# Activation tables loaded ahead, two norms moved to VectorE, and three constants of the planner, in a hybrid decoder layer on eight cores

## The reference

```
h      = rmsnorm(x) @ w_in                       # 1024 -> 512 + 512 + 512 + 1024 + 1024
a      = h[:, :512];  u, v = gelu(h[:, 512:1536])
p      = (causal window sums of a, windows 2, 4, 8, 16, minus a) @ w_pool, per group
s      = u * (causal 128x128 mix of rmsnorm(v) by w_s + b_s)
merged = sigmoid(gate_a) * (p @ w_pool_out) + sigmoid(gate_b) * (s @ w_gmlp_out)
x      = x + merged @ w_out
h2     = rmsnorm(x)
x      = x + (silu(h2 @ w_gate) * (h2 @ w_up)) @ w_down      # d_ff 2816
y      = rmsnorm(x)
```

## Time and profile before

| | us |
|---|---|
| median of 3 runs (776.41 to 777.02) | 776.97 |
| the profiled execution, its own time | 777.7 |
| its span on the slowest core, core 5 | 776.1 |
| spans of the other cores | 771.0 to 776.0 |
| TensorE busy | 742.0 (96%) |
| DVE, ACT, POOL busy | 538.4, 354.5, 107.2 |

### The profile page before, as it was taken

How to read it: one execution, slowest core, us unless ns; L and a number is a source line. 1 busy time by engine, 2 the same in 40 slices (tenths; PEclk the granted TensorE clock), 3 DMA queues, 4 the chain that set the end, 5 groups by cost and what they waited for, 6 DMA issues and landing times.

```text
span 776.1 us, 14774 instructions; the slowest of 8 cores (771.0 to 776.1 us)
## 1 busy us (share of the span) xinstructions
PE 742.0 (96%) x4855; PEld 435.8 (56%) x4855; DVE 538.4 (69%) x1164; ACT 354.5 (46%) x753; POOL 107.2 (14%) x185
## 2 busy tenths in 40 slices
PE   5999999999999999999999999999999999999995
PEld 2664555666666654446656665445665666654442
DVE  2788868667666656766568758965577566768986
ACT  3587654544444445675545552001554555531222
POOL 4245111001000011120121001000111000002111
PEclk9999999999999999999999999999999999999998
DMA  8998704015223249573599205861385332005652
GB/s 204 242 246 187 159 27 57 1 15 82 42 29 42 28 86 281 123 142 90 94 197 139 36 10 76 271 213 29 55 133 91 50 42 42 1 1 186 224 192 109
DMA packets 46715, 82.92 MB, mean 107 GB/s; under 512 B 20288, under 2 KB 20416, under 8 KB 46624
## 3 DMA queue, kind: packets, MB, share of 16 engines
q0 software_dynamic: 15984, 29.11, 26.0%
q1 hardware_dynamic: 30222, 52.28, 23.0%
q10 hardware_dynamic: 434, 0.60, 0.2%
HBM read 87.83 MB, written 19.49 MB: 138 GB/s over the span
## 4 chain that ended last, share of the span: by engine, by line
PE 76%; issue 6%; DVE 6%; ACT 5%; DMA 4%; POOL 2%; DVEq 0%; ACTq 0%; POOLq 0%
PE ps L546 74%; ACT junk L567 3%; POOL rs L691 2%; DMA Sx<-wpk 2%; DMA Rg<-wpk 2%; DVE X L578 2%; ACT Sx L567 1%; DVE Pr L578 1%; ACT Fr L567 1%; DVE X L586 1%; PE ps L723 1%; DMA Mr<-wpk 1%; PE ps L1071 1%; DVE hT L578 1%; DVE Sx L578 0%
## 5 line engine op out<-in xcount | busy, mean ns | idle before, releaser
L567 ACT ACTIVATE Fr<-ps 128x344 f32<-128x344 f32 (+2 forms) x394 | 180.2, 465 | 203.0 <-PE ps L546 188.0
L578 DVE TENSOR_TENSOR Fr<-Fr,ps 128x344 f32<-128x344 f32 (+2 forms) x366 | 179.7, 508 | 109.0 <-ACT Fr L567 71.5
L546 PE MATMUL ps<-hT,Rg 128*128 128x344 f16 x1440 | 245.8, 309 | 5.5 <-ACT Fr L567 5.5
L546 PE MATMUL ps<-Sx,Rg 128*128 128x344 f16 x1080 | 189.9, 309 | 2.3 <-DVE Fr L578 1.5
L546 PEld LDWEIGHTS ps<-hT,Rg 128*128 128x128 f16 x1440 | 139.4, 98 | 78.8 <-issue 11.0
L546 PEld LDWEIGHTS ps<-Sx,Rg 128*128 128x128 f16 x1080 | 103.2, 98 | 59.3 <-issue 10.3
L578 DVE TENSOR_TENSOR X<-X,ps 128x512 f32<-128x512 f32 (+1 forms) x121 | 80.5, 682 | 26.0 <-PE ps L546 23.6
L567 ACT ACTIVATE Fr<-Fr 128x344 f16<-128x344 f32 x138 | 67.3, 488 | 54.5 <-DVE Fr L578 52.6
L546 PE MATMUL ps<-Mr,Pr 128*128 128x512 f16 x352 | 82.0, 379 | 2.4 <-DVE X L578 2.2
L611 POOL DMA_DIRECT2D Rg<-wpk x60 | 31.9, 532 | 374.5 <-PE ps L546 374.1
L567 ACT ACTIVATE junk<-X 128x1025 f16<-128x1025 f32 (+3 forms) x43 | 43.9, 1022 | 78.3 <-DVE X L578 73.1
(11 more groups left out here) (116 smaller groups left out, 575.6 us busy)
## 6 DMA issues: line engine op xcount, KB each, us to landing
Rg<-wpk POOLq DMA_DIRECT2D x60, 256.0 KB, 4.9
X<-xp SPq DMA_DIRECT2D x22, 512.0 KB, 13.4
X<-xd SPq DMA_DIRECT2D x18, 512.0 KB, 4.7
Mr<-wpk POOLq DMA_DIRECT2D x34, 256.0 KB, 8.7
yp<-X SPq DMA_DIRECT2D x14, 512.0 KB, 2.9
xd<-Pr SPq DMA_DIRECT2D x12, 512.0 KB, 6.1
Pr<-xp SPq DMA_DIRECT2D x10, 512.0 KB, 10.2
xd<-X SPq DMA_DIRECT2D x8, 512.0 KB, 5.4
```

What stands on the lines that cost most here:

```text
L546: ins = e.matmul(out=ap, lhsT=l, rhs=rr, start=(start and i == 0), stop=(stop and i == len(pairs) - 1), skip_group_check=more)
L567: return e.activation(out=P.r(out), in_=P.r(in_), func=func, scale=scale, **kw)
L578: return P.add(eng, lambda e: e.tensor_tensor(out=P.r(out), in0=P.r(a), in1=P.r(b), op=op), reads=[a, b], writes=[out], dur=vdur(n, per), ...
```

## The change

Five edits.

- Before the gate stage one activation of eight elements with Sigmoid is added on ACT, to run after all GELUs; all sigmoids run after it. Before the FFN one with SiLU, after all sigmoids; the SiLUs run after it. Both have priority -8 and are planned at 1400 ns.
- The power step of `rstd` is planned at 850 ns with a delay of 300 for priorities of 100 and more (560 and 150 before), and at 560 with 200 below.
- The first two norms are scaled on DVE, as the others are.
- Weights with a priority under 0.35 (the a, v and u units) count as landed 1000 ns later in the plan.
- A queue that turns active while the other has work is held for the full `LAG` in the plan.

```diff
+HSL = 1000.0
...
         if not self.q[i]:
-            self.gate[i] = self.t + min(self.left(1 - i), LAG)
+            self.gate[i] = self.t + (LAG if self.q[1 - i] else 0.0)
...
-                fin.done = rings.t + LAND
+                fin.done = rings.t + LAND + fin.slack
...
         def load(u, ap, sem, prio, after=()):
             where[u] = ap
-            return dma('pool', ap, wpk[UIDX[u], :, :], sem, rows(128, 4096), prio, after)
+            o_ = dma('pool', ap, wpk[UIDX[u], :, :], sem, rows(128, 4096), prio, after)
+            o_.slack = HSL if prio < 0.35 else 0.0
+            return o_
...
-                  dur=560.0, lat=150.0, prio=-6.0)
+                  dur=(560.0 if prio < 100.0 else 850.0), lat=(200.0 if prio < 100.0 else 300.0), prio=-6.0)
...
-        sca = lambda t: t < 2
+        sca = lambda t: False
...
+        gelus = []
+        sigs = []
+
+        def table(func, done):
+            o_ = act(tmp16[0:1, 0:8], mhalf[0:1, 0:1].to_broadcast([1, 8]), func, -8.0, n=8)
+            o_.dur = 1400.0
+            o_.preds = sorted(set(o_.preds) | set(q.i for q in done))
+            return o_
+
+        def follow(o_, pre):
+            o_.preds = sorted(set(o_.preds) | {pre.i})
+            return o_
...
+        sig0 = table(AF.Sigmoid, gelus)
...
-                    act(h[2], v, AF.Sigmoid, pr, n=WJ)
+                    sigs.append(follow(act(h[2], v, AF.Sigmoid, pr, n=WJ), sig0))
...
-                    act(s, t, AF.Sigmoid, pr, n=WJ)
+                    sigs.append(follow(act(s, t, AF.Sigmoid, pr, n=WJ), sig0))
...
+        sil0 = table(AF.Silu, sigs)
...
-                    act(h[0], t1, AF.Silu, pr, n=WJ)
+                    follow(act(h[0], t1, AF.Silu, pr, n=WJ), sil0)
...
-                    act(h[2], v, AF.Silu, pr, n=WJ)
+                    follow(act(h[2], v, AF.Silu, pr, n=WJ), sil0)
```

More of the change, by code:

```diff
@@ L92 @@
     __slots__ = ('i', 'eng', 'fn', 'dur', 'lat', 'prio', 'preds', 'succs', 'npred', 'pts', 'alloc',
-                 'dma', 'nbytes', 'start', 'end', 'done', 'seq', 'clock', 'waits', 'val', 'margin', 'loose')
+                 'dma', 'nbytes', 'start', 'end', 'done', 'seq', 'clock', 'waits', 'val', 'margin', 'loose', 'slack')
 class Rings:
@@ L200, in add @@
         o.loose = loose
+        o.slack = 0.0
         o.pts = []
@@ L796, in v_tile @@
             fv[0] = 1 - fi
-            act(Fb[:R, fi, 0:512], PV(pt, lambda p: p[:R, :]), AF.Gelu_apprx_tanh, prio)
+            gelus.append(act(Fb[:R, fi, 0:512], PV(pt, lambda p: p[:R, :]), AF.Gelu_apprx_tanh, prio))
             r = rstd(Fb[:R, fi, 0:513], R, 512.0 ** -0.5, prio)
@@ L822, in u_sample @@
             fs = Fb[:, fi, 0:64]
-            act(fs, PV(pt, lambda p: p[:, 0:64]), AF.Gelu_apprx_tanh, prio, n=64)
+            gelus.append(act(fs, PV(pt, lambda p: p[:, 0:64]), AF.Gelu_apprx_tanh, prio, n=64))
             def trs(e, p):
@@ L860, in u_stage @@
             fu[0] = 1 - fu[0]
-            act(Fb[:, fi, :W], PV(pt, lambda p: p[:, :W]), AF.Gelu_apprx_tanh, prio)
+            gelus.append(act(Fb[:, fi, :W], PV(pt, lambda p: p[:, :W]), AF.Gelu_apprx_tanh, prio))
             ps = PT()
@@ L1134, in build_nc @@
                 xstore(t, 2200.0 + n_, tlast)
-        fs = [0]
+        sil0 = table(AF.Silu, sigs)
         def ffn_unit(row, j, B, pr):
```

## The result

The changed kernel takes 768.06 us (median), the kernel before 776.69 in the same comparison: the ratio is 0.9882, 95% interval 0.9864 to 0.9899, so 1.2% faster, which is 9.2 us by the ratio; the two medians are 8.6 apart. The forecast was 773.2 with a range down to 769.5. The direction was right, the size was not: more than twice the gain. All comparisons are with runs of the kernel before on the same chip. Ratios, intervals and means of spans leave out the runs in which some cores ran at a lower clock and took some per cent longer; medians are over all runs.

What follows compares the result with a forecast made beforehand. TensorE's own work was taken to set the time, so only its standstills could change it. Sigmoid 1.0, SiLU 1.28, start 1.5 and power step 0 summed to 3.8 us, from 776.97 to 773.2; range 769.5 to 776.7.

Steps and rivals of the forecast that it cites:

- Sigmoid: Gate start: table load leaves the stretch between sum and first sigmoid; 1.0 us of TensorE's 1.30 us wait gained.
- SiLU: FFN start: table load moves behind the last sigmoid, copies come earlier; 1.28 us of TensorE's 2.83 us wait gained.
- The row and the page: Table loads: trace rows show 1.28 us per switch; the skill's page adds a 1.38 us drain, 2.66 in all.
- Start: First stage: norms on DVE, later weights and queue rule bring tile 1 earlier and remove TensorE's waits; 1.5 us gained.
- The rival that has the start given back: First stage paced by transfers, so only the tables pay: 2.3 us gained, 774.7 us; chance 0.24.
- Power step: Tail: longer planned step doesn't flip the order; taken at 0, with up to 1.9 us gained or lost.
- The larger gain by more flips: FFN start and tail: SiLU and copies precede the last scaling, three tail waits go; 7.3 us, 769.7; chance 0.10.
- ACT parked on x: First stage: squares planned ahead of copies make ACT wait for x, 3.9 us each; two give 781.0; chance 0.10.
- Renamed waits: Gate, FFN and first stage: other waits replace those removed; about 0.5 us gained, 776.5; chance 0.14.

Runs made afterwards that it cites:

- e17: The kernel before with the SiLU table activation alone; 775.04 us, ratio 0.9953.
- e18: The kernel before with 15 matmuls put on TensorE ahead of the group that waits at the FFN's start; 776.36 us, ratio 0.9983.
- e4: The kernel before with the three first-stage edits alone (norms on DVE, weights later, held queue rule); 777.60 us, ratio 0.9999.
- e2: The kernel before with the longer planned power step alone; 771.93 us, ratio 0.9928.
- e14: The kernel before with the power step planned longer in the FFN's final norm alone; 775.00 us, ratio 0.9965.
- e15: The kernel before with the power step planned as in the full change everywhere but in the final norm; 774.36 us, ratio 0.9950.
- e13: The kernel before with both table activations and the longer planned power step, without the three first-stage edits; 768.80 us, ratio 0.9887.
- e3: The kernel before with both table activations (Sigmoid and SiLU) alone; 772.67 us, ratio 0.9933.
- e1: The changed kernel with the power step planned as before (560 ns, delay 150); 773.64 us, ratio 0.9946.
- e16: e13 with the power step planned at 1460 ns instead of 850 for priorities of 100 and more; 767.09 us, ratio 0.9856.

## Why the prediction was right and wrong

**Sigmoid: right.** Taken at 1.0, measured 1.23 on all cores. The cover that I named, four groups on pooled data, is there. The table load moved behind the first copy, not ahead of it, so even the later copy for which I set 0.3 aside didn't come.

**SiLU: the mechanism right, the term mis-sized.** "So of 2.83 us I take 1.28." It measured 2.9 in the mean of the spans (e17): the wait itself fell by 1.43, a wait for a tile before it by 0.30, and the clock behind it gave back about 1 us more (e18). I had read one core, on which the clock didn't fall; the metric takes the slowest of eight. The upper end of 2.83, by which SiLU and copies come before the last scaling, didn't come: they stand behind it in every kernel.

The row and the page that I set against each other are told apart by this: the two loads are worth 1.23 and 1.43 us where the load stood, next to 1.28 for the load by itself. The Trainium skill ("ScalarE: Activation LUTs", "What ACT_TABLE_LOAD costs") puts a load at 2.66 with a drain of 1.38; no run here shows the drain.

**Start: wrong.** "The two together should take away the waits for activations, 0.83 + 0.69 = 1.5 us." It gave nothing (e4), and the waits themselves stayed, 0.82 and 1.18 on core 0 of after. Tile 1 came earlier, but the step from there to the u weights failed: I held 1.8 us to be free by the landing of one weight, while the squares on ACT wait for x, and through them the copies, TensorE at 31.86, and the first use of the weight, which is not before 38.5 but at 38.8 in after and 39.3 in e4. The rival that has the start given back was right on the start; its total of 774.7 was not. That old and new rule agree for the rest of the program, as I assumed, held: kernels with and without the start edits have the same lists behind the first 103 us.

**Power step: the step that failed.** "The order does not flip, so I take 0, with up to 3 x 0.65 = 1.9 gained or as much lost." It was worth 5.1 to 5.6 us alone (e2). I compared when the scaling is due with one thing, the addition behind it, and the addition indeed didn't pass it. The planner compares the scaling with everything that is ready on DVE, and a sum for a later group was: laid out 0.44 us later, the scaling comes behind that, and TensorE's order changes with it (e14, 2.2 us). I also set the times of the trace against each other where the planner has its own; in those the margin was 0.04 us, and had the step been planned 0.05 shorter, TensorE's order and my 0 would have stood in the tail. The fourth wait there, 1.42 us, I didn't see. And I looked for the effect in the tail alone, while the same step stands before the scalings of the first stage and the second norm (2.9 us, e15).

**Rivals.** The larger gain by more flips, at one chance in ten, had the mechanism in the tail, with 769.7 as its time; the flip at the FFN's start, SiLU and copies ahead of the scaling, is not how the rest came. ACT parked on x had its mechanism too: it happens in every kernel with the start edits. But its price was too high: with up to 12.2 us of such waits, and all else that the start edits do, e4 isn't slower. Renamed waits is right for the start alone. The sum of what was measured, Sigmoid 1.2, SiLU 2.9 and the power step 5.1, is 9.2 and by chance the same as the measured gain: the parts share 1.3 of it, and the changed kernel has 1.3 less than e13, of which 0.8 are the last stores. The mean of the spans fell by 9.7.

## What to carry to other kernels

Where a static planner lays out the order, look at waits on an operation whose estimate is below what the trace shows (0.56 planned, 0.71 on average, 1.46 beside DVE): other ready work may stand behind it. Correct the estimate for that operation alone and look at every place where it stands, not at the largest. Such a planner needs no chip: play it through with the new estimate and compare the orders of all engines before you put a term at 0, and mind how near a flip is to not happening. Price a long wait of TensorE at more than its length when the work behind it runs at a lower granted clock on any core, and look at all cores for that, since the slowest sets the time. A lead at the start of a stage is no gain until it reaches the stage's end: follow it through what the stage waits for, here the landing of x as well as of the weights.

## What was not expected of the hardware

The clock of TensorE differed between cores that ran the same instructions with the same wait: behind 2.8 us of idleness it fell on 13 of 24, behind 2.4 us on 7 of 16. A second such place is near 73 us, where the mix of the u stage waits for DVE twice in short order; on core 7 of the kernel before TensorE's waits there are 1.15 and 0.33 us, and the next 4 us have a granted clock of 0.57:

```profile
74.08 0.38 PE L546 MATMUL ps<-Mr 128*128 128x512 f16 x1 [1.15 <-DVE Pr L578]
74.79 2.15 PE L546 MATMUL ps<-Mr 128*128 128x512 f16 x6 [0.33 <-DVE Pr L578]
```

```profile
75.00:79.00 4.00, 4.00 (x12) 1.33 (x11) 2.08 (x4) 4.00 (x9) 2.11 (x4) 0.57 1.01 204
```

Waits of this kind there (1.15 to 1.19 and 0.33 to 0.38 us) are followed by the lower clock on 7 of the 40 cores of before, e3, e14, e17 and e18, two of them in the kernel before (1.5 to 1.7 us each), and on none of the 56 of the other kernels with a profile (after, e1, e2, e4, e13, e15 and e16). In e2 and e15 that may be part of the gain of the longer power step; it is read from the traces and no run tried it by itself.

The last two stores land in 2.1 to 2.5 us in seven kernels and in 2.9 to 3.7 in five, with the same order of work in front of them.
